# Attention pair and head schedule of a hybrid decoder step: sinks and bias made a pair ahead, PE's last turns reordered, head scores regrouped, prologue interleaved

## The reference, cut to what matters

```python
xn = rmsnorm(x, norm_in)
qa, fa, ia, za, qb, kb, vb, zb, ga, gb = in_projection(xn, w_in)
q, k, v, logf = hgrn2_features(qa, fa, ia, lb)      # branch A: 8 heads of 128
oa, S_new = hgrn_fn(q, k, v, logf)                  # chunked gated recurrence
ob, ck, cv = swa_fn(qb, kb, vb, b_sinks)            # branch B: 16 query heads, 2 kv heads, window 128
hb = ob * silu(zb)
...
s = einsum('bnqhgd,bnshd->bnhgqs', qb, kk) * scale  # scores against own and previous block
s = s - alibi_slopes(...) * dist                    # bias: slope of the head times the distance
p = sink_softmax(s, sinks)                          # softmax with one more logit per head, the sink
o = einsum('bnhgqs,bnshd->bnqhgd', p, vv)
```

## Time and profile before

| what | us |
|---|---|
| median of three timed runs | 1361.92 |
| the profiled execution's own time | 1358.19 |
| its span, first to last instruction | 1356.4 |
| PE busy / DVE busy / ACT busy / POOL busy | 1303.2 / 600.2 / 515.3 / 261.7 |

### The profile page before, as it was taken

How to read it: one execution, slowest core, us unless ns; L and a number is a source line. 1 busy time by engine, 2 the same in 40 slices (tenths; PEclk the granted TensorE clock), 3 DMA queues, 4 the chain that set the end, 5 groups by cost and what they waited for, 6 DMA issues and landing times.

```text
span 1356.4 us, 23483 instructions
## 1 busy us (share of the span) xinstructions
PE 1303.2 (96%) x9148; PEld 1229.1 (91%) x9148; DVE 600.2 (44%) x1237; ACT 515.3 (38%) x1019; POOL 261.7 (19%) x119
## 2 busy tenths in 40 slices
PE   5799999999999999999999999999999899999998
PEld 4799999999999999999999988888888899999885
DVE  6546465565647474510000055556555401445222
ACT  6343536344443534521111245545444413213111
POOL 0222222212122222132212111111011022342000
PEclk9899999999999999999999999999999999999999
DMA  6201121212020212111112311110110312151231
GB/s 192 65 25 53 51 65 33 62 33 76 18 77 17 77 33 73 39 50 43 46 46 51 82 32 31 31 28 18 31 31 1 88 47 62 32 124 32 97 132 43
DMA packets 136750, 73.61 MB, mean 54 GB/s; under 512 B 37185, under 2 KB 133138, under 8 KB 136690
## 3 DMA queue, kind: packets, MB, share of 16 engines
q1 hardware_dynamic: 136706, 72.99, 19.5%
HBM read 63.77 MB, written 10.22 MB: 55 GB/s over the span
## 4 chain that ended last, share of the span: by engine, by line
PE 56%; issue 27%; DVE 8%; POOL 6%; ACT 2%; DMA 1%; DVEq 0%; SPq 0%; POOLq 0%; ACTq 0%
PE pj L966 39%; POOL w_l L556 5%; PE pj L982 3%; DVE scores L1604 3%; PE pj L1326 2%; PE ps_a L1326 1%; PE ps_e L1326 1%; PE ps_e L1203 1%; PE ps_d L1203 1%; PE ps_d L1326 1%; PE ps_b L1326 1%; PE ps_c L1326 1%; DVE scores L1592 1%; PE ps_c L1191 1%; PE ps_b L1191 1%
## 5 line engine op out<-in xcount | busy, mean ns | idle before, releaser
L966 PE MATMUL pj<-xn_h,w_h 128*128 128x352 f32 x1704 | 563.3, 331 | 14.4 <-DVE q L1397 5.5
L966 PE MATMUL pj<-xn_h,w_l 128*128 128x352 f32 x1704 | 552.1, 324 | 0.0
L966 PE MATMUL pj<-xn_l,w_h 128*128 128x352 f32 x1704 | 551.5, 324 | 0.0
L966 PEld LDWEIGHTS pj<-xn_h,w_h 128*128 128x128 f32 x1704 | 323.6, 190 | 23.4 <-issue 9.4
L556 POOL TENSOR_TENSOR w_l<-w_raw,w_h 128x1024 fp32r<-128x1024 f32 x82 | 204.0, 2488 | 710.2 <-ACT w_h L628 710.1
L966 PEld LDWEIGHTS pj<-xn_l,w_h 128*128 128x128 f32 x1704 | 324.8, 191 | 0.1
L966 PEld LDWEIGHTS pj<-xn_h,w_l 128*128 128x128 f32 x1704 | 323.9, 190 | 0.0
L628 ACT ACTIVATE w_h<-w_raw 128x1024 fp32r<-128x1024 f32 x82 | 86.6, 1056 | 114.7 <-PE pj L966 100.2
L1559 DVE TENSOR_TENSOR mg<-sg,pj 128x352 f32 (+1 forms) x24 | 12.4, 521 | 152.0 <-PE pj L966 150.6
L833 ACT ACTIVATE scores<-scores,stat 128x256 f32<-128x256 f32 (+1 forms) x128 | 61.6, 486 | 0.0
L966 PE MATMUL pj<-hl_l,w_h 128*128 128x352 f32 x168 | 54.2, 323 | 0.0
(11 more groups left out here) (362 smaller groups left out, 2069.9 us busy)
## 6 DMA issues: line engine op xcount, KB each, us to landing
w_raw<-in_w_in_dram SPq DMA_DIRECT2D x132, 256.0 KB, 3.3
x_t<-in_x_prompt_dram SPq DMA_DIRECT2D x8, 512.0 KB, 8.9
s<-in_state_hgrn_dram SPq DMA_DIRECT2D x8, 512.0 KB, 4.3
out_dram<-s SPq DMA_DIRECT2D x8, 512.0 KB, 3.2
w_raw<-in_w_pa_dram SPq DMA_DIRECT2D x16, 256.0 KB, 3.0
w_raw<-in_w_pb_dram SPq DMA_DIRECT2D x16, 256.0 KB, 4.5
wo_raw<-in_w_out_dram SPq DMA_DIRECT2D x8, 512.0 KB, 4.0
x_o<-in_x_prompt_dram SPq DMA_DIRECT2D x8, 512.0 KB, 4.2
```

The source lines that it names most:

```text
L966: mm = nc.tensor.matmul(pj[g][:, 0:W], w[:, kt, :], x[:, kt, span(g)], start=(kt == 0 and m == 0), stop=(kt == KT - 1 and m == 2))
```

## The change

The program makes the same values. On PE, the head's eight 64-wide score products stand together ahead of all 32-wide ones. In a pair, `turn(7)` stands before `out(5)`, and the last gate slot after `out(7)`. On DVE, the sinks and the bias of pair m+1 are made in pair m, behind the normalisation (those of pair 0 while the values are projected); the copy `z_s` moves behind the normalisation; `h0` moves ahead of the last copied turn; and in the prologue the three products `q0` to `q2` stand between the exponents instead of behind them.

```diff
-    softmax = (["b0", "b1", "sk", "qs"] + [x for k in quarters for x in units("t", k) + [f"nm0_{k}", f"nm1_{k}"]] + ["zs"]
+    softmax = (["qs"] + [x for k in quarters for x in units("t", k) + [f"nm0_{k}", f"nm1_{k}"]]
...
                         nc.tensor.matmul(bank[0:64, o + 64:o + 128], d64[:, c, 0, :], d64[:, c, 1, :], start=True, stop=True)
+                for n, bank in enumerate((ps_a, ps_b)):
+                    for j in range(4):
+                        c, o = 4 * n + j, j * P
                         for m in range(2):
...
                 out(4)
+                turn(7)
                 out(5)
-                turn(7)
-                gate_slot(2)
                 out(6)
                 out(7)
+                gate_slot(2)
...
                 v.tensor_tensor_scan(b[:], reset[:], b[:], 0.0, ALU.mult, ALU.add).then_inc(dve_done, done("scan"))
+                if now[0] == "pro":
+                    gated(pr, "q", 0, q)
...
                 tt(kD[:, SEQ:T].rearrange("p (b t) -> p b t", b=NB), ...).then_inc(dve_done, done("kDs"))
+                if now[0] == "pro":
+                    gated(pr, "q", 1, q)
...
+                if now[0] == "pro":
+                    gated(pr, "q", 2, q)
                 bd = b[:, 0:SEQ].rearrange("p (c t) -> p c t", t=32)
...
             exponents_of(pr, 0)
-            for g in range(SLOTS):
-                gated(pr, "q", g, q)
...
+            def slopes_of(now, m):
+                v.tensor_copy(sink_m[:]..., sinks[:]...[:, :, bass.ds(m, 1)]).then_inc(dve_done, dve.tick(now, "sk"))
+                for h in range(2):
+                    v.tensor_scalar(bias[:, h, :], dist[:], slopes[:, bass.ds(m + 8 * h, 1)], None, ALU.mult).then_inc(dve_done, dve.tick(now, f"b{h}"))
+
+            v.wait_ge(dve_done, dve.at(here, "sel1"))
+            slopes_of(here, 0)
             v.wait_ge(pe_done, pe.at(here, "vt1"))
...
-                for h in range(2):
-                    v.tensor_scalar(bias[:, h, :], dist[:], slopes[:, bass.ds(m + 8 * h, 1)], None, ALU.mult).then_inc(dve_done, dve.tick(now, f"b{h}"))
...
+                v.wait_ge(dve_done, dve.at(prev, "h1"))
                 v.wait_ge(pe_done, pe.at(now, "s0"))
-                v.tensor_copy(sink_m[:]..., sinks[:]...[:, :, bass.ds(m, 1)]).then_inc(dve_done, dve.tick(now, "sk"))
-                v.wait_ge(dve_done, dve.at(now, "b1"))
                 v.tensor_copy(q_s[:, :, bass.ds(m, 1), :], ...).then_inc(dve_done, dve.tick(now, "qs"))
...
-                v.tensor_copy(z_s[:, bass.ds(m, 1), :], one(zb[:, SEQ:T])).then_inc(dve_done, dve.tick(now, "zs"))
                 for k in quarters:
                     normalise(now, k, stat, QU * k, QU * (k + 1), scores, keys)
+                v.tensor_copy(z_s[:, bass.ds(m, 1), :], one(zb[:, SEQ:T])).then_inc(dve_done, dve.tick(now, "zs"))
+                if not last:
+                    slopes_of(now, m + 1)
...
+                copy_turned(1)
+                copy_turned(3)
+                copy_turned(5)
+                gated_values(0)
+                copy_turned(7)
+                gated_values(1)
```

More of the change, by code:

```diff
@@ L108, in hybrid_step @@
     exps = [x for k in quarters for x in [f"es0_{k}", f"es1_{k}"] + units("p", k)]
-    softmax = (["b0", "b1", "sk", "qs"] + [x for k in quarters for x in units("t", k) + [f"nm0_{k}", f"nm1_{k}"]] + ["zs"]
-               + [x for k in quarters for x in [f"dn{k}", f"rd{k}"] + units("n", k)])
-    turn_order = ["t0", "t1", "t2", "o0", "o1", "t3", "t4", "o2", "o3", "t5", "t6", "o4", "o5", "t7", "o6", "o7"]
+    softmax = (["qs"] + [x for k in quarters for x in units("t", k) + [f"nm0_{k}", f"nm1_{k}"]]
+               + [x for k in quarters for x in [f"dn{k}", f"rd{k}"] + units("n", k)] + ["zs"])
+    values = ["pt1", "pt3", "pt5", "h0", "pt7", "h1"]
+    turn_order = ["t0", "t1", "t2", "o0", "o1", "t3", "t4", "o2", "o3", "t5", "t6", "o4", "t7", "o5", "o6", "o7"]
     norms = ["rl0", "rl1", "rls", "rx"]
@@ L141, in hybrid_step @@
         ("pro", ["par", "lbm", "lbd0", "lbd1", "lbs", "lbr", "lb", "oml", "noml", "mean"] + per_tile(["xn"], ["lo_a", "lo_b"])
-         + ["att0", "atts0", "reset", "reset_p", "reset_s"] + exponents + each_slot("q") + each_slot("z"), 1, 0),
+         + ["att0", "atts0", "reset", "reset_p", "reset_s"]
+         + exponents[:2] + ["q0"] + exponents[2:4] + ["q1"] + exponents[4:8] + ["q2"] + exponents[8:] + each_slot("z"), 1, 0),
         ("head", ["ha"] + products + chain + masked + exponents + ["q0"] + gated_head
@@ L147, in hybrid_step @@
         ("pa", each_slot("m"), HEADS, 0),
-        ("kv", ["sel0", "sel1", "vt1"] + each_slot("z"), 1, 0),
-        ("swa", softmax + ["pt1", "pt3", "pt5", "pt7", "h0", "h1"] + each_slot("z"), HEADS - 1, 0),
-        ("swa_l", softmax + ["pt1", "pt3", "pt5", "pt7", "h0", "h1"], 1, 0),
+        ("kv", ["sel0", "sel1", "sk", "b0", "b1", "vt1"] + each_slot("z"), 1, 0),
+        ("swa", softmax + ["sk", "b0", "b1"] + values + each_slot("z"), HEADS - 1, 0),
+        ("swa_l", softmax + values, 1, 0),
         ("swa_s", ["ct1"] + units("t", 0) + ["nm0_0", "nm1_0", "dn0", "rd0"] + units("n", 0) + ["pn", "h"], 1, 0),
@@ L1570, in _ @@
                                        op0=ALU.mult, op1=ALU.add, accum_out=sinks_s[:, h:h + 1]).then_inc(dve_done, dve.tick(here, f"sel{h}"))
+            def slopes_of(now, m):
+                v.tensor_copy(sink_m[:].rearrange("p (h m) -> p h m", h=2), sinks[:].rearrange("p (h m) -> p h m", h=2)[:, :, bass.ds(m, 1)])\
+                 .then_inc(dve_done, dve.tick(now, "sk"))
+                for h in range(2):
+                    v.tensor_scalar(bias[:, h, :], dist[:], slopes[:, bass.ds(m + 8 * h, 1)], None, ALU.mult).then_inc(dve_done, dve.tick(now, f"b{h}"))
+            v.wait_ge(dve_done, dve.at(here, "sel1"))
+            slopes_of(here, 0)
             v.wait_ge(pe_done, pe.at(here, "vt1"))
@@ L1594, in pair @@
             def pair(m):
-                now = pair_of(m)
+                now, prev = pair_of(m), ("swa", m - 1)
                 last = is_last(m)
                 keys = lambda u: slice(P if u < 2 else 0, 2 * P)
-                for h in range(2):
-                    v.tensor_scalar(bias[:, h, :], dist[:], slopes[:, bass.ds(m + 8 * h, 1)], None, ALU.mult).then_inc(dve_done, dve.tick(now, f"b{h}"))
                 def biased(u):
@@ L1606, in biased @@
                                            accum_out=stat[:, 0, u:u + 1]).then_inc(dve_done, dve.tick(now, f"t{u}"))
+                v.wait_ge(dve_done, dve.at(prev, "h1"))
                 v.wait_ge(pe_done, pe.at(now, "s0"))
-                v.tensor_copy(sink_m[:].rearrange("p (h m) -> p h m", h=2), sinks[:].rearrange("p (h m) -> p h m", h=2)[:, :, bass.ds(m, 1)])\
-                 .then_inc(dve_done, dve.tick(now, "sk"))
-                v.wait_ge(dve_done, dve.at(now, "b1"))
                 v.tensor_copy(q_s[:, :, bass.ds(m, 1), :], qT[:, SEQ:T].rearrange("p (b o t) -> p b o t", b=NB, o=1)).then_inc(dve_done, dve.tick(now, "qs"))
@@ L1618, in pair, with copy_turned @@
                            lambda h: sink_m[:, h:h + 1], scores_next=k + 1)
-                v.tensor_copy(z_s[:, bass.ds(m, 1), :], one(zb[:, SEQ:T])).then_inc(dve_done, dve.tick(now, "zs"))
                 for k in quarters:
                     normalise(now, k, stat, QU * k, QU * (k + 1), scores, keys)
-                for n in range(1, NC, 2):
+                v.tensor_copy(z_s[:, bass.ds(m, 1), :], one(zb[:, SEQ:T])).then_inc(dve_done, dve.tick(now, "zs"))
+                if not last:
+                    slopes_of(now, m + 1)
+                def copy_turned(n):
                     v.wait_ge(pe_done, pe.at(now, f"t{n}"))
@@ L1625, in pair, with gated_values @@
                         v.wait_ge(pe_done, pe.at(now, f"o{n - 3}"))
-                    src = (ps_a, ps_b, ps_c)[n % 3]
-                    v.tensor_copy(PT[:, n % 3, :, :].rearrange("p a q -> p (a q)"), src[:]).then_inc(dve_done, dve.tick(now, f"pt{n}"))
-                for n, bank in enumerate((ps_d, ps_e)):
+                    v.tensor_copy(PT[:, n % 3, :, :].rearrange("p a q -> p (a q)"), (ps_a, ps_b, ps_c)[n % 3][:]).then_inc(dve_done, dve.tick(now, f"pt{n}"))
+                def gated_values(n):
                     v.wait_ge(pe_done, pe.at(now, f"o{4 * n + 3}"))
-                    tt(hb[:, bass.ds(m, 1), half(n)], one(bank[:]), one(zb[:, half(n)]), ALU.mult).then_inc(dve_done, dve.tick(now, f"h{n}"))
+                    tt(hb[:, bass.ds(m, 1), half(n)], one((ps_d, ps_e)[n][:]), one(zb[:, half(n)]), ALU.mult).then_inc(dve_done, dve.tick(now, f"h{n}"))
+                copy_turned(1)
[4 more added lines that the diff above has]
+                gated_values(1)
                 if not last:
```

## The result

The changed kernel took 1328.26 us as the median of four timed runs (1327.93 to 1329.06), the kernel before 1361.41 beside it, now of four runs (1357.56 to 1361.92): a ratio of 0.977, 95% interval 0.9758 to 0.9782. The forecast was 1333.7 in a range of 1324 to 1345. The profiled execution took 1327.93 us, against 1358.19 before: 30.3 us less, where the sum said 28.2.

What follows compares the result with a forecast made beforehand. PE is busy 96% of the span, so only its waits and drains can be won. Prologue 8.0, heads 7.2 and pairs 13.0 sum to 28.2 us: 1361.92 less that is 1333.7 us, range 1324 to 1345.

Steps and rivals of the forecast that it cites:

- Prologue, 8.0: Before block 2: 5.5 us of PE idling for q and 2.5 us of slow slot go; bounds 5.5 to 8.2.
- Heads, 7.2: Head score blocks: grouping 64-wide products saves drains at width changes, 0.9 us a head in eight heads.
- Grouped, a 64-wide product is two records at 0.11, 0.21: Head scores: two records 0.11 us apart make 0.21 per 64-wide product, giving 0.33 to 0.42 per chunk for 0.51.
- The bounds of 0 to 10: Limits in us on the heads' gain; 0 if the drains return as something else.
- The rival that the heads give nothing: Head scores: a floor between starts or one busy strip keeps blocks near 4 us; 1340.9 us, chance 0.17.
- the slower one: Head scores: grouped products queue in one column strip at full duration, 49 us lost against 21 won; 1390, chance 0.03.
- Pairs, 13.0: Branch B: pairs 1 to 6 start like pair 0, 1.81 us each (10.9), pair 7 2.1; bounds 7.0 to 17.5.
- PE's wait at turn(2): In each pair: PE still waits for n5 from DVE's chain tied to score(2); a wait of 0.3 us left.
- wait for copied turns: Pairs: 0.85 us of new DVE work delays copies by 0.1 to 0.2 us; a wait above 0.5 disproves a step.
- the negation took over POOL's block: Pair start: the first negation, not the sinks' copy, meets POOL's op and takes 1.5 us, at no cost to PE.
- Clock, 3.4 either way: Four of eight heads lose 1.7 us each to a low-clock stretch; which heads can shift, so 3.4 us either way.
- Heads at 0.6 and the clock against it: Case given for the forecast's own upper bound: heads gain only 0.6 us each and the clock is unfavourable; about 1345 us.

Runs made afterwards that it cites:

- the sinks back: Changed kernel with sinks and bias made at the start of their own pair again, PE's new order kept: 1327.78 us, ratio 0.9771.
- PE's old order: Changed kernel with the last gate slot ahead of out(6) and out(7) again, turn(7) behind out(5), sinks and bias still a pair ahead: 1330.21 us, ratio 0.9778.
- the changed kernel's second run: The changed kernel as it is, run again in the second set of experiments for comparison: 1327.51 us (1326.72 to 1328.45).

## Why the prediction came out, step by step

**Prologue, 8.0: right.** 8.2 us from the last slot of block 0 to the head's scores, the upper bound; the idle 5.5 and the slow slot both went.

**Heads, 7.2: the term that was mis-sized.** The step that failed is "Grouped, a 64-wide product is two records at 0.11, 0.21": the 0.11 was read from the only pair there was, which stood right behind a change of width. In the changed kernel the first gap is still 0.106, and all others are 0.058. So eight 64-wide products take 1.07 us with the change behind them, not 1.7, and the 32-wide ones 1.13, inside what was forecast for them. The block takes 2.20 for 4.06: 1.86 less a head, 14.9 in eight. Of these, 14.1 arrived. Two more low stretches than before, six for four, at 0.74 us net of the POOL wait that each one hides, would explain a loss of 1.5; the difference is within what single heads differ by. The bounds of 0 to 10 did not hold the value: a price seen once in a mixed stretch is not an upper bound for a pure one.

96 of the 32-wide records started in 92.31 - 91.18 = 1.13 us, 12 ns each. The Trainium skill (TensorE: Matmul & The Clock Gate, section "Wait — 56ns, not 53.3ns?") states that matmuls never start less than about 25 ns apart. The trace does not agree for these tiles; by that floor they would take 2.4 us, an estimate.

The rival that the heads give nothing is refuted, and so is the slower one: sixteen 64-wide records on one strip took 1.07 us, where full durations one behind another would take 16 x 0.222 = 3.6.

**Pairs, 13.0: right in size, the reason only half.** Six pairs gave 37.42 - 35.75 = 1.67 each (1.81 forecast), pair 7 gave 2.4 (2.1), and pair 0 lost 0.14, which had been left out: 12.2. The runs put the loss in pair 0 on PE's order and not on the copies made ahead: pair 0 takes 35.77 with the sinks back and 35.50 with PE's old order. As forecast, PE's wait at turn(2) stayed at 0.28, no wait for copied turns showed, the sinks' copy fell to 0.16 us, and the negation took over POOL's block at 1.32 (1.5 forecast), with POOL's op over 3.97 us into pair 1 (about 4 forecast). But the prediction told both edits as needed. The runs with one of them undone show that either alone gives more than four fifths, because DVE was late by one block beside POOL and by one late start together, and PE's slack covers either of them.

**Clock, 3.4 either way: right that it moves, too narrow by a little.** It cost 3.1 us behind the sample attention, a place that the prediction did not name, and some 1.5 in the heads. The price behind the sample attention is seen once more: from the first score of pair 7 to the start of the last matmul the changed kernel's second run took 311.8 us with a low stretch of 6.83 us, the one with the sinks back 308.9 without. In the heads a stretch cost less than the 1.7 us of the prediction: 1.27 over a head of 60.17 that has neither a low stretch nor the wait for POOL, and 0.74 over one that has the wait.

Why the clock falls in the sample attention in some runs and not in others is not settled. The small products there were not spread.

**The range: its upper end does not follow from its words.** Heads at 0.6 and the clock against it give 1361.92 - 8.0 - 4.8 - 13.0 + 3.4 = 1339.5; near 1345 takes the lower bounds of the prologue and the pairs as well. The result lies far from that end, so nothing hangs on it.

## What to carry to other kernels

Price a regrouping from the gaps inside a run of one tile width, and if none exists in the trace, take the change's price off every gap next to one. Two edits that cure the same lateness do not add: ask of each what is late without the other. And before trusting a small difference, count the low stretches of the clock: a loop whose length falls into step with them pays in every turn, and spreading its thinnest matmuls among full ones gave 6.7 us in the heads here.

## What the runs showed of the hardware

A return from 32-wide to 64-wide tiles and back costs about 0.27 us in both layouts (1.86 us for seven, and 2.47 - 2.20 for one). Grouped 64-wide records start 0.058 us apart on one column strip while each is recorded as 0.222 long; 32-wide ones over four strips start 0.012 apart. Sixteen records of 4 columns in a row on the whole array took 1.81 us, 0.113 each, almost what the 128-column ones take (0.111), and in six of eight heads the clock fell to half in the slot behind them. With the same products put between the 128-column ones it fell in none of sixteen heads of two kernels, though the products took as long: the six records of a chunk started within 0.67 us (166.70 to 167.37), 0.112 each.
